# Compression's steps moved up in the last mixer of a two-block network on one core

## The chip, the cores and the metric

One core of one Trainium2 chip. The metric is the time of one execution on the device, in microseconds.

## What is computed

Two blocks run one after the other on a sequence of 256 tokens of width 1024, in float32. The first has two layers (feed-forward, hybrid mixer, feed-forward). The second has two layers of a mixer and a feed-forward; its second mixer, which the change touches, is sparse attention beside a conformer branch. Cut to what matters here:

```python
def compress_blocks(tok, pos_emb, w1, w2):
    n_cmp = (t - CMP_BLOCK) // CMP_STRIDE + 1      # blocks of 32 tokens, stride 16: 15 of them
    blocks = tok[:, :, idx] + pos_emb
    return jax.nn.gelu(blocks.reshape(...) @ w1) @ w2

def sparse_attn_conformer_mixer(h, w_in, ...):
    u = h @ w_in
    q, kc, vc, ks, vs, kw, vw, gt, cf = jnp.split(u, offs, axis=-1)
    # native_sparse_attention:
    q  = apply_rope(rms_norm(q, q_norm), cos, sin)
    ks = apply_rope(rms_norm(k_slc, k_norm[0]), cos, sin)
    kw = apply_rope(rms_norm(k_win, k_norm[1]), cos, sin)
    kc_tok = apply_rope(k_cmp, cos, sin)
    kc = rms_norm(compress_blocks(kc_tok, cmp_pos[0], cmp_w1[0], cmp_w2[0]), k_norm[2])
    vc = compress_blocks(v_cmp, cmp_pos[1], cmp_w1[1], cmp_w2[1])
    # scores of q against kc, ks, kw; softmax of each; three outputs, gated and added
    a, b = jnp.split(cf, 2, axis=-1)
    z = causal_dwconv(a * jax.nn.sigmoid(b), conf_dw) + conf_dw_b
    z = jax.nn.silu(layer_norm_2(z, conf_ln_g, conf_ln_b))
    return jnp.concatenate([o_nsa, z], axis=-1) @ w_out
```

## The kernel before

**One program, five engines.** The class Walk goes through the network once for each engine and calls the same steps in the same order; each engine's program (TensorProgram on TensorE or PE, ScalarProgram on ScalarE or ACT, VectorProgram on VectorE or DVE, GpsimdProgram on GpSimd or POOL, SyncProgram for the weight loads) issues its own part of a step, or nothing. So the place of a call in Walk is the order on every engine at once. Each engine works strictly in that order; semaphores hold a step until what it needs is there.

**Matrix products.** A float32 weight is loaded in units of 2 x 128 rows (RW, 512 KB at most), split by ACT into a high part WH (line 922) and by DVE into the rest WL (line 1266); the input has both parts too (XT), and each product is three matmuls (lines 446 to 451). These splits are called cuts. Units are loaded four ahead and cut up to five ahead (LEAD is 4); there are six places for cut units. `rows` yields after each of 8 pieces of 6 matmuls of 512 columns, `cols` with steps=2 after each of 8 pieces of 12 matmuls of 256 columns. The loop around it calls one entry of the list `beside` at each yield. So these lists set what stands between the pieces.

**The last mixer, mixer_odd.** It projects the compressed branch's keys and values, rotates the keys (`rotate("c", ...)`) and stores them to device memory (`keys_out`). `windows` (POOL, line 2095) waits for those stores, reads them back as pairs of neighbouring tokens into PRS with four loads (line 2101), and clears FB (line 2105). `paired` turns the pairs on PE (line 779) and adds the position table on DVE into FB (line 1821). `hidden` is compression's first layer: 64 matmuls on PE (line 791), Gelu on ACT (line 1179). `hidden_turn` is lines 800 and 1185, `compressed_rows` its second layer (line 825), with the norm of the compressed keys on ACT and DVE (lines 1201 to 1208, 1829 to 1838, result KCN), `compressed_keys` turns these (PE line 834, ACT line 1213, result KCT).

`rotate(kind, t, ...)` for the keys k and the queries q is a norm and a rotation: square on ACT (line 1151), sum on DVE (1781), square root on ACT (1154), six steps on DVE (1783 to 1804), two products on POOL (2072, 2074) that DVE needs at lines 1800 and 1804. `odd_q` copies q to SBUF (ACT, line 1173). `keys_double` copies the rotated keys twice into KD on POOL (line 2111); `clear_vcb` clears a table there (2116) once line 791 is done. `features` turns KD and the rotated q on PE (line 813) and copies them out on ACT (line 1192). `odd_gate` is the sigmoid of the conformer's gates, SGc (line 1160). After that a loop of ticks runs the attention items: `cmp_scores` (PE 844, DVE 1845 to 1851, exponentials on ACT, line 1221), PE 866, ACT 978, DVE 1902, PE 875, and `upper`, the conformer's upper half, whose gated result ZC (DVE, line 1811) is stored and read back shifted (POOL 2122, 2131) for the convolution (PE, line 768).

**Order around the change.** In the loop over q's eight pieces come the two rotations of k, then `windows`, then `paired(0)` and `paired(1)` at the end. In the loop over the gates' eight pieces come q's first rotation, `hidden`, `keys_double` and q's second rotation, `hidden_turn`, `features` of k, `compressed_rows`, nothing, `features("q", 0)`. `compressed_keys` is called in the second tick.

Of the kernel before, what the change touches and what calls it, by code (L numbers as in the profile page):

```python
# [2221 lines left out]
class Walk:  # L2222
# [681 lines left out]
    def mixer_odd(self):  # L2904
        k, e = self.k, self.e
# [24 lines left out]
        def rotate(kind, t, h0, h1, normed):  # L2930
            e.rotate(kind, t, h0, h1, normed, [("odd_v", ("ro", kind, 0))] if t else [])
# [7 lines left out]
        for t in range(2):  # L2939
            e.odd_win(t, bks[t])  # L2940
            self.drop(bks[t], ("odd_a", ("win", t)))

        def paired(n):
            b = self.bank()
            e.paired(n, b)
            self.drop(b, ("odd_v", ("fb", n)))

        def features(kind, t):
            b = self.bank()
            e.features(kind, t, b)  # L2950
            self.drop(b, ("odd_a", ("qkt", kind, t)))
# [17 lines left out]
        def compressed_keys():  # L2969
            b = self.bank()  # L2970
            e.cmp_keys(b)
            self.drop(b, ("odd_a", "kct"))
# [1 line left out]


        bks = [self.bank(), self.bank()]
        beside = [lambda: rotate("k", 0, 8, 12, 12), e.nothing, lambda: rotate("k", 1, 8, 12, 12), e.windows, e.nothing,
                  e.nothing, lambda: paired(0), lambda: paired(1)]
        for _ in self.rows(w, 8, 0, [(0, 512, bks)], self.x):
            beside.pop(0)()  # L2980
        for t in range(2):
# [3 lines left out]


        bks = [self.bank() for _ in range(4)]
        beside = [lambda: rotate("q", 0, 0, 8, 8), hidden, lambda: (e.keys_double(), e.clear_vcb(), rotate("q", 1, 0, 8, 8)),
                  hidden_turn, lambda: (features("k", 0), features("k", 1)), compressed_rows, e.nothing,
                  lambda: features("q", 0)]  # L2990
        for _ in self.cols(w, 1816, 4, bks, self.x, steps=2):
            beside.pop(0)()
        for j in range(4):
# [70 lines left out]
        def convolve():  # L3064
            for j in range(4):
                if j % 2 == 0:
                    b = self.bank()
                for p in range(8):
                    e.conv_taps4(j, p, b)
                    if p % 4 == 3 and 2 * j + p // 4 + 2 < 8:  # L3070
                        e.conv_weights(2 * j + p // 4 + 2)
                    if p == 7 and j % 2:
                        e.conv_sum(j - 1, b)
                        self.drop(b, ("odd_a", ("za", j)))
                    yield

        def conformer(t):
            b = self.bank()
            e.conf_turn(t, b)
            e.conf_norm(t)  # L3080
            self.drop(b, ("odd_v", ("zn", t)))
            yield
            yield
            b = self.bank()
            e.conf_back(t, b)
            self.drop(b, ("odd_a", ("zs", t)))
            yield

        def upper():

            for half in range(2):
                bks = [self.bank(), self.bank()]
                yield from self.cols(w, 1304 + 256 * half, 2, bks, self.x)
                for j in range(2):
                    e.odd_up(2 * half + j, bks[j])
                    self.drop(bks[j], ("odd_v", ("zc", 2 * half + j)))
                e.conv_out(half)
                e.conv_shift(half)
# [7 lines left out]
        up, conv, live, tick, ticks = upper(), convolve(), [], 0, 0  # L3106
        outs = 0
        while gens or live or conv:
            while gens and tick >= gens[0][0]:
                tick = 0 if gens[0][0] else tick  # L3110
                live.append(gens.pop(0)[1])
            tick += 1
            ticks += 1
            if ticks == 2:
                compressed_keys()
            if ticks == 4:
                features("q", 1)
                later["q1"] = True
            live = [g for g in live if next(g, self) is not self]
            if up:  # L3120
                if next(up, self) is self:
                    up = None
            elif conv:
                for _ in range(2):
                    if conv and next(conv, self) is self:
                        conv = None
                        live += [conformer(0), conformer(1)]
            elif outs < 4 and len(done[0]) == 4 or outs < 8 and len(done[1]) == 4:
                outs += 1
                next(y)  # L3130
# [147 lines left out]
```

## Time and profile before

| | |
|---|---|
| median of 3 runs | 2339.42 us (2338.87 to 2340.22) |
| span of the profiled execution | 2339.1 us |
| PE busy | 2277.7 us, 97% of the span |
| DVE, ACT, POOL busy | 1485.2, 1164.7, 128.7 us |
| chain that ended last, by engine | PE 86%, DVE 8%, ACT 4%, DMA 1% |

Only the span is given for the profiled execution, no time of its own; the median of the runs stands 0.3 us above that span. An engine's busy time says little by itself here. To read it: see where PE stood idle, who released it, and what that engine was doing before.

### The profile page before, as it was taken

What the parts mean: (1) busy time and instruction counts of PE and PEld (TensorE: products, weight loads), DVE (VectorE), ACT (ScalarE), POOL (GpSimd) and SP (SyncE); (2) the same over time, 40 slices, a digit from 0 to 9 for tenths busy, and PEclk for the clock granted to TensorE, in tenths of its full rate; (3) what the DMA queues carried; (4) which work ended last, traced back from release to release, by engine and by line L of the source; (5) the groups of instructions that cost most, each with busy time, mean ns of one, the idle gap of its engine ahead of it and who ended that gap; (6) DMA issues with size and microseconds to landing.
All of it is one profiled execution on the core that took longest, in us unless ns stands there. A gap on an engine that the chain in (4) does not pass through costs nothing.

```text
span 2339.1 us, 33502 instructions
## 1 busy us (share of the span) xinstructions
PE 2277.7 (97%) x13839; PEld 1929.1 (82%) x13839; DVE 1485.2 (63%) x2139; ACT 1164.7 (50%) x1799; POOL 128.7 (6%) x197
## 2 busy tenths in 40 slices
PE   8999999999999999999999999999989999788999
PEld 7888798887888878888898877888878887666887
DVE  5665567857666556664668667666467664565663
ACT  5554346534555436553356344555344553545652
POOL 2100010120000000000000110000000001320000
PEclk9999999999999999999999999999999999889999
DMA  6756473445565556566544446566535665442663
GB/s 220 228 187 214 146 226 113 133 127 188 180 191 187 190 187 199 185 203 201 175 153 132 136 145 206 180 192 209 193 122 189 182 211 175 131 129 84 205 192 132
DMA packets 283560, 408.09 MB, mean 174 GB/s; under 512 B 13700, under 2 KB 170688, under 8 KB 283152
## 3 DMA queue, kind: packets, MB, share of 16 engines
q1 hardware_dynamic: 275600, 380.91, 51.1%
q0 software_dynamic: 7808, 25.04, 3.6%
q8 instruction: 109, 1.79, 0.3%
q14 instruction: 43, 0.35, 0.0%
HBM read 403.98 MB, written 1.91 MB: 174 GB/s over the span
## 4 chain that ended last, share of the span: by engine, by line
PE 86%; DVE 8%; ACT 4%; DMA 1%; issue 1%; POOL 0%; SPq 0%; DVEq 0%; ACTq 0%; POOLq 0%
PE PS L517 23%; PE PS L449 13%; PE PS L451 12%; PE PS L450 12%; PE PS L516 10%; PE PS L446 2%; DVE WL L1266 2%; PE PS L448 2%; PE PS L447 2%; PE PS L519 1%; PE PS L466 1%; ACT WH L922 1%; DVE QX L1513 1%; DMA RW<-in_w_in_odd 1%; PE PS L661 0%
## 5 line engine op out<-in xcount | busy, mean ns | idle before, releaser
L1266 DVE TENSOR_TENSOR WL<-RW,WH 128x1024 fp32r<-128x1024 f32 (+2 forms) x732 | 870.8, 1220 | 314.9 <-ACT WH L922 312.4
L922 ACT ACTIVATE WH<-RW 128x1024 fp32r<-128x1024 f32 (+2 forms) x732 | 740.6, 1044 | 389.0 <-PE PS L451 223.2
L517 PE MATMUL PS<-XT,WH 128*128 128x512 f32 x2368 | 808.4, 394 | 0.0
L516 PE MATMUL PS<-XT,WL 128*128 128x256 f32 x2072 | 580.5, 280 | 0.0
L517 PEld LDWEIGHTS PS<-XT,WH 128*128 128x128 f32 x2368 | 425.1, 188 | 76.7
L516 PEld LDWEIGHTS PS<-XT,WL 128*128 128x128 f32 x2072 | 390.0, 188 | 13.3
L449 PE MATMUL PS<-WH,HTH 128*128 128x512 f32 x688 | 271.4, 394 | 0.0
L451 PE MATMUL PS<-WH,HTL 128*128 128x512 f32 x688 | 270.8, 394 | 0.0
L450 PE MATMUL PS<-WL,HTH 128*128 128x512 f32 x688 | 269.7, 392 | 0.0
L449 PE MATMUL PS<-WH,XT 128*128 128x512 f32 (+4 forms) x640 | 252.4, 394 | 8.5 <-DVE SX L1420 3.3
L451 PE MATMUL PS<-WH,XT 128*128 128x512 f32 (+4 forms) x640 | 243.2, 380 | 0.0
L450 PE MATMUL PS<-WL,XT 128*128 128x512 f32 (+4 forms) x640 | 242.4, 379 | 0.0
L446 PE MATMUL PS<-XT,WH 128*128 128x256 f32 x560 | 164.4, 294 | 2.5 <-DVE Z L1400 1.3
L449 PEld LDWEIGHTS PS<-WH,XT 128*128 128x128 f32 x640 | 123.3, 193 | 43.4 <-issue 10.7
L447 PE MATMUL PS<-XT,WL 128*128 128x256 f32 x560 | 158.4, 283 | 0.0
L448 PE MATMUL PS<-XT,WH 128*128 128x256 f32 x560 | 158.3, 283 | 0.0
L451 PEld LDWEIGHTS PS<-WH,HTL 128*128 128x128 f32 x688 | 129.1, 188 | 30.7
L450 PEld LDWEIGHTS PS<-WL,HTH 128*128 128x128 f32 x688 | 129.1, 188 | 30.2
L1336 DVE TENSOR_TENSOR HM<-PS,HM 128x256 f32<-128x256 f32 x148 | 62.3, 421 | 144.2 <-ACT HM L952 144.2
L449 PEld LDWEIGHTS PS<-WH,HTH 128*128 128x128 f32 x688 | 129.2, 188 | 28.9
L952 ACT ACTIVATE HM<-PS 128x256 f32<-128x256 f32 x148 | 56.8, 384 | 178.4 <-PE PS L517 174.1
L952 ACT ACTIVATE SG<-PS 128x256 f32<-128x256 f32 x148 | 56.9, 385 | 175.5 <-PE PS L517 174.7
(438 smaller groups left out, 2556.1 us busy)
## 6 DMA issues: line engine op xcount, KB each, us to landing
RW<-in_w_ff_in SPq DMA_DIRECT2D x256, 512.0 KB, 4.4
RW<-in_w_ff_out SPq DMA_DIRECT2D x128, 512.0 KB, 4.5
RW<-in_w_in SPq DMA_DIRECT2D x56, 512.0 KB, 4.5
RW<-in_w_gate SPq DMA_DIRECT2D x48, 512.0 KB, 4.2
RW<-in_ffn_gate SPq DMA_DIRECT2D x44, 512.0 KB, 4.3
RW<-in_ffn_up SPq DMA_DIRECT2D x44, 512.0 KB, 4.5
RW<-in_ffn_down SPq DMA_DIRECT2D x44, 512.0 KB, 4.6
RW<-in_w_out SPq DMA_DIRECT2D x16, 512.0 KB, 4.7
```

The lines of the kernel that those rows point to most:

```text
L446: self.e.matmul(o, wh, xh, start=start, stop=False)
L447: self.e.matmul(o, wl, xh, start=False, stop=False)
L448: return self.e.matmul(o, wh, xl, start=False, stop=stop)
L449: self.e.matmul(o, xh, wh, start=start, stop=False)
L450: self.e.matmul(o, xh, wl, start=False, stop=False)
L451: return self.e.matmul(o, xl, wh, start=False, stop=stop)
L516: self.e.matmul(k.PS[:, b.n, 0:T], wl, k.XTH[:, kt, :], start=False, stop=False)
L517: ins = self.e.matmul(k.PS[:, b.n, :], wh, k.XT[:, kt, :], start=kt == 0, stop=kt == 7)
L922: self.e.activation(u.hi_out, raw, ACT.Copy).then_inc(*self.s["hi"].up(u.n))
L952: self.e.activation(f[2 + part][:, n, j * T:j * T + T], self.k.PS[:, b.n, 0:T], ACT.Copy).then_inc(*self.s["ffn_a"].up((seq, sl, n, part, j)))
L1266: self.e.tensor_tensor(u.lo_out, raw, u.hi_out.bitcast(F), ALU.subtract).then_inc(*self.s["lo"].up(u.n))
L1336: self.e.tensor_tensor(v, self.k.PS[:, b.n, T:2 * T], v, ALU.add).then_inc(*self.s["ffn_v"].up((seq, sl, n, part, j)))
```

## The change

Five calls move; nothing is added to or taken from the work.

- `windows` is called right after the window branch's values are copied (`odd_win`), ahead of both rotations of k, where it was behind them.
- `paired(0)` and `paired(1)` come one piece earlier each, and `hidden` is called after the last piece of q, ahead of `odd_q` and of all the gates' pieces.
- `hidden_turn`, `features` of k and `compressed_rows` come one or two pieces earlier in the loop over the gates.
- `compressed_keys` is called at the end of that loop, ahead of `odd_gate`, where it was in the second tick behind it.

```diff
@@ -2939,6 +2939,7 @@
         for t in range(2):
             e.odd_win(t, bks[t])
             self.drop(bks[t], ("odd_a", ("win", t)))
+        e.windows()
 
@@ -2974,8 +2975,8 @@
         bks = [self.bank(), self.bank()]
-        beside = [lambda: rotate("k", 0, 8, 12, 12), e.nothing, lambda: rotate("k", 1, 8, 12, 12), e.windows, e.nothing,
-                  e.nothing, lambda: paired(0), lambda: paired(1)]
+        beside = [lambda: rotate("k", 0, 8, 12, 12), e.nothing, lambda: rotate("k", 1, 8, 12, 12), e.nothing, e.nothing,
+                  lambda: paired(0), lambda: paired(1), hidden]
         for _ in self.rows(w, 8, 0, [(0, 512, bks)], self.x):
             beside.pop(0)()
@@ -2985,9 +2986,9 @@
         bks = [self.bank() for _ in range(4)]
-        beside = [lambda: rotate("q", 0, 0, 8, 8), hidden, lambda: (e.keys_double(), e.clear_vcb(), rotate("q", 1, 0, 8, 8)),
-                  hidden_turn, lambda: (features("k", 0), features("k", 1)), compressed_rows, e.nothing,
-                  lambda: features("q", 0)]
+        beside = [lambda: rotate("q", 0, 0, 8, 8), hidden_turn, lambda: (e.keys_double(), e.clear_vcb(), rotate("q", 1, 0, 8, 8)),
+                  lambda: (features("k", 0), features("k", 1)), compressed_rows, e.nothing, e.nothing,
+                  lambda: (features("q", 0), compressed_keys())]
         for _ in self.cols(w, 1816, 4, bks, self.x, steps=2):
             beside.pop(0)()
@@ -3111,8 +3112,6 @@
             tick += 1
             ticks += 1
-            if ticks == 2:
-                compressed_keys()
             if ticks == 4:
```

DVE's order is the same before and after. On POOL, in the projection of q (TM are the products of k's rotation, PRS the pairs, W_150 compression's second weights):

```order
 L2083 DMA W_150<-in_cmp_w_2 128x4x64
+L2101 DMA PRS<-scratch 128x2x64 x4
+L2105 MEMSET FB_133 128x1024
+L2105 MEMSET FB_134 128x1024
 L2072 TENSOR_TENSOR TM_137<-RT_131,CO 128x128
 L2074 TENSOR_TENSOR TM_138<-RT_131,CO 128x128
 L2072 TENSOR_TENSOR TM_137<-RT_132,CO 128x128
 L2074 TENSOR_TENSOR TM_138<-RT_132,CO 128x128
-L2101 DMA PRS<-scratch 128x2x64 x4
-L2105 MEMSET FB_133 128x1024
-L2105 MEMSET FB_134 128x1024
```

The four loads and two clears pass four products.

On ACT, between q's projection and the gates' (G_140 is Gelu's output, RT the copies of q, RO their squares, SX at line 1154 the square root):

```order
 L922 ACTIVATE WH<-RW 128x2x512 x2
+L1179 ACT_TABLE_LOAD
+L1179 ACTIVATE G_140<-PS 128x256
 L1173 ACTIVATE RT_131<-PS 128x512
 L1173 ACTIVATE RT_132<-PS 128x512
 L922 ACTIVATE WH<-RW 128x2x256
 L1151 ACTIVATE RO_135<-RT_131 128x512
-L1154 ACTIVATE SX<-SX,ST 128x8
-L1179 ACT_TABLE_LOAD
-L1179 ACTIVATE G_140<-PS 128x256
```

Gelu and its table load pass both copies of q, a cut, a square and a root.

On ACT, at the end of the gates' projection (QTT is q's copy, KCT the compressed keys', SGc the gates, the table load of line 1221 is the exponentials'):

```order
 L1192 ACTIVATE QTT<-PS 128x4x128
+L1213 ACTIVATE KCT<-PS 128x64
 L1160 ACT_TABLE_LOAD
 L1160 ACTIVATE SGc<-PS 128x256 x4
 L922 ACTIVATE WH<-RW 128x2x256
-L1213 ACTIVATE KCT<-PS 128x64
 L1221 ACT_TABLE_LOAD
```

The keys' copy passes the gates and a cut.

## Rows read from the trace of the kernel before

**Rows 1.** The page's head and its busy times
```profile
span 2339.1 us, 33502 instructions
...
PE 2277.7 (97%) x13839; PEld 1929.1 (82%) x13839; DVE 1485.2 (63%) x2139; ACT 1164.7 (50%) x1799; POOL 128.7 (6%) x197
```
**Rows 2.** Timeline of PE: start, us, instruction; in brackets the idle time before it
```profile
2014.55 0.66 PE L779 MATMUL PS<-CO,PRS 128*128 128x128 f32 x2 [12.25 <-DMA PRS<-scratch]
...
2021.77 7.13 PE L791 MATMUL PS<-W,FB 128*64 128x256 f32 x64
...
2073.49 1.94 PE L768 MATMUL PS<-Z,DG 128*32 128x256 f32 x16 [4.24 <-issue]
```
**Rows 3.** Timeline of POOL
```profile
1992.59 0.75 POOL L2083 DMA_DIRECT2D W<-in_cmp_w  x1
...
2011.43 2.89 POOL L2101 DMA_DIRECT2D PRS<-scratch  x4
...
2022.35 0.96 POOL L2072 TENSOR_TENSOR TM<-RT,CO 128x256 f32<-128x256 f32 x1 [6.18 <-DVE RT L1788]
...
2023.94 1.56 POOL L2111 COPY KD<-RO 128x512 f32<-128x512 f32 x2
```
**Rows 4.** DMA issues: KB, us to landing (1989.2:1990.1, 1992.3:1993.5, 2011:2015)
```profile
scratch<-VV POOLq DMA_DIRECT2D x1, 64.0 KB, 3.9
...
W<-in_cmp_w POOLq DMA_DIRECT2D x1, 128.0 KB, 10.4
...
PRS<-scratch POOLq DMA_DIRECT2D x4, 64.0 KB, 2.5
```
**Rows 5.** Timeline of DVE
```profile
2012.08 2.35 DVE L1266 TENSOR_TENSOR WL<-RW,WH 128x1024 fp32r<-128x1024 f32 x2
2015.39 0.66 DVE L1821 TENSOR_TENSOR FB<-PS,VEC 128x480 f32<-128x480 f32 x1 [0.95 <-POOL FB L2105]
...
2025.06 0.72 DVE L1804 TENSOR_TENSOR RO<-RO,TM 128x256 f32<-128x256 f32 x1
...
2036.27 0.51 DVE L1804 TENSOR_TENSOR RO<-RO,TM 128x256 f32<-128x256 f32 x1
...
2039.11 0.29 DVE L1829 TENSOR_REDUCE SX<-KCN 128x2 f32<-128x128 f32 x1 [1.52 <-ACT KCN L1205]
...
2040.61 0.23 DVE L1838 COPY KCN<-KCN 128x128 f32<-128x128 f32 x1
```
**Rows 6.** Timeline of ACT
```profile
2020.28 0.30 ACT L1154 ACTIVATE SX<-SX,ST 128x8 f32<-128x8 f32 x1 [0.84 <-DVE SX L1781]
...
2028.95 0.38 ACT L1179 ACTIVATE G<-PS 128x256 f32<-128x256 f32 x1 [7.07 <-PE PS L791]
...
2031.68 0.30 ACT L1154 ACTIVATE SX<-SX,ST 128x8 f32<-128x8 f32 x1
...
2041.54 1.28 ACT L1160 ACT_TABLE_LOAD   x1
2042.83 1.21 ACT L1160 ACTIVATE SGc<-PS 128x256 f32<-128x256 f32 x4
...
2046.75 0.96 ACT L1221 ACTIVATE PCM<-PCM,SX 128x32 f32<-128x32 f32 x4 [0.78 <-DVE SX L1851]
...
2054.58 0.60 ACT L1192 ACTIVATE QTT<-PS 128x512 f32<-128x512 f32 x1 [0.39 <-PE PS L813]
```
**Rows 7.** Stretches: us, busy of PE, PEld, DVE, ACT, POOL, granted PE clock, DMA
```profile
2014.50:2019.90 5.40, 5.35 (x19) 4.69 (x20) 2.26 (x4) 1.63 (x3) 1.67 (x2) 0.50 0.43 123
...
2028.90:2040.90 12.00, 12.00 (x105) 12.00 (x105) 7.35 (x16) 7.86 (x17) 6.06 (x11) 1.00 0.18 45
...
2042.50:2044.80 2.30, 0.03 (x1) 0.02 (x1) 0.21 (x1) 2.27 (x8) 0.00 (x0) 1.00 0.44 112
...
2047.30:2054.10 6.80, 6.80 (x32) 6.51 (x32) 4.11 (x13) 2.32 (x8) 0.00 (x0) 0.51 0.34 126
```
**Rows 8.** The chain that ended last: start, us, what
```profile
2032.13 0.12 PE PS L446
```

## Prediction

> **What bounds the kernel now.** I read the page's busy table first, then TensorE's timeline through the last mixer, then the timelines of the three engines that it waits for, then the clock. The profiled execution spans 2339.1 us with TensorE busy 97% of it [rows 1], so only places where TensorE stands still, or runs at its lower clock, can give or take time. The last mixer has four such places [rows 2, 7]. PE waits 12.25 us before the transposes of the token pairs (line 779). It waits 2.3 us for the compressed keys before line 844. It waits 4.24 us before the conformer's convolution (line 768). And after the first two of these it works for 5.4 and 6.8 us at half the clock (granted 0.50 and 0.51, the 1.2 GHz level).
>
> The 12.25 us are a queue, not a transfer. The four loads of PRS are issued on POOL at 2011.43, because the products of the keys' rotation stand ahead of them there [rows 3]; the four landed 2.5 us after their issue at the median [rows 4]. So the change aims at a real wait. The question is what stands behind it.
>
> **The change, step by step.** No instruction is added or removed; all is order.
>
> 1. *Pairs earlier.* The loads now follow W2's load, issued at 1992.59 [rows 3]. They wait for the keys' own stores, of which the last was issued by 1990.1 and took 3.9 us [rows 4], so they begin at 1994.0. Four issues of 0.72 us, 2.89 us in all [rows 3], end at 1997.0. When they land the trace doesn't show. The nearest rows bound it: 2.5 us after issue as in a quiet time, 1999.5, and 10.4 us as W2's load took just ahead of them in the same queue, 2007.4 [rows 4]. I take 2005.5, behind W2's landing at 2003.0, since these loads stand in that queue. PE then does the two pairs' transposes and the last 12 matmuls of 512 columns in what was idle time. In turn they may delay the weight loads beside them: by nothing, or by as much as the 2.5 us that they took themselves [rows 4]. I take nothing, because they stand behind W2's load, and the weights of this stretch were asked for earlier.
>
> 2. *The hidden layer's start.* Its 64 matmuls (line 791) now follow at once, ahead of the 24 matmuls that used to stand between. But they need FB, and FB is written on DVE, whose order did not change: rotation of the keys, two cuts of weights (2012.08 and 2.35 long), then two additions of 0.66 us [rows 5]. So they start at 2014.4 + 2 x 0.66 = **2015.8**, not when the pairs land: 6.0 us sooner than 2021.77 [rows 2], not 12. PE has then waited some 6 us more and starts at the lower clock. At full clock the 64 took 7.13 us [rows 2]; as in [rows 7] I take 5.4 us at half clock, which loses 2.7. They end at 2015.8 + 7.1 + 2.7 = **2025.6**, 3.3 us sooner than 2028.9. Bounds: no loss, 2022.9, and a 6.8 us stretch, 2026.3.
>
> 3. *What the early wait on ACT costs.* Gelu (line 1179) used to stand behind the copies of q (line 1173) and the start of q's first rotation. It now stands ahead of them. ACT is in order, so it waits for line 791 before the copies, and both rotations of q, of which the first used to run beside line 791 (root at 2020.28, last DVE step ended 2025.78 [rows 5, 6]), begin after it. From Gelu to the root of a rotation took 2031.68 - 2028.95 = 2.73 us [rows 6]; two copies of q come in between, 0.6 each less an overlap of 0.1 (the copy of this size in [rows 6]), 3.73. So the root of q's first half is at 2029.4, its rotation ends 5.5 us later (as before) at 2034.9. Two DVE passes of 0.6 each (a cut and the next sum, each of about FB's size, 0.66, less their overlap) put the second root at 2036.1; that half took 2036.78 - 2031.68 = 5.1 us [rows 5, 6] and ends at 2041.2. One more cut, 0.6, and the norm of the compressed keys, 2039.11 to 2040.84, 1.73 us [rows 5]: the keys are ready at **2043.5**. Before it was 2040.84. Here the gain of step 2 is already gone.
>
> 4. *PE in that stretch.* After line 791 it has 12.0 us of work as in [rows 7] plus the 24 matmuls that moved behind it, 24 x 0.12 = 2.9 [rows 8]. In it the keys' features (line 813) are now asked for after four pieces of 12 matmuls and two transposes, 50 x 0.12 = 6.0 us, at 2031.6. They need KD from POOL, whose two copies follow q's products in order. Products 2.07 us after the root (2020.28 to 2022.35), copies 1.59 us later, 0.8 each [rows 3, 6]: first copy done at 2033.9, second at 2034.7. So PE **waits 2.3 us, then 0.4 us more**, where it waited for nothing before. Its work ends at 2025.6 + 14.9 + 2.7 = 2043.2, just ahead of the keys. But a wait of this very length, 2.30 us, was followed by a half-clock stretch that lost 3.4 us (6.8 at 0.51), and the first wait by one that lost 2.7 [rows 7]. Bounds: 0 and 3.4. I take 2.7, nearest to both: the compressed keys are turned at **2045.9**.
>
> 5. *Keys ahead of gates.* Before, ACT ran gates' table load, gates, a cut and then the keys' copy; the exponentials started at 2046.75, held by DVE and not by ACT. Now the gates stand between keys' copy and exponentials: q's copy 0.5, keys' copy 0.15 (an eighth of its size, mostly fixed cost), table load 1.28, gates 1.22, a cut of the copy's size 0.5, table load 1.28 [rows 6], 5.0 us after the turn: **2050.9**, 4.1 us later. The scores' own steps on PE and DVE fit into these 5 us and are no longer what is waited for. On from there ACT and DVE are a chain: the cut, the sums, the second exponentials, q's second copy, which had waited 0.39 us for PE [rows 6]. That slack is used up first: 4.1 - 0.4 = 3.7. This chain ends in ZC on DVE, whose transfers hold the convolution; the 4.24 us that PE waited there [rows 2] are filled by a slower PE but not by a later ZC. The work behind goes with it.
>
> A rule on ACT is worth weighing. In [rows 6] a table load starts at 2041.54, takes 1.28 us and the gates follow at 2042.83, so a switch costs 1.28. The Trainium skill ("ScalarE: Activation LUTs", What ACT_TABLE_LOAD costs) puts a switch at about 2.66 us, a drain included. By it the two switches of step 5 would bring 2.8 us more, and the sum would be 2345.9. The trace shows no drain behind the load, so the sum goes by the row.
>
> **Sum.** +3.5 us, rounded down from 3.7 for overlaps. The span of 2339.1 becomes 2342.6; the median of the runs stands 0.3 above the span, so the forecast is **2342.9 us**. A measurement of this kernel can tell about 0.2%, 4.7 us, from no change (2334.7 to 2344.1); the forecast lies inside.
>
> **Rivals.**
>
> *The clock holds* (0.20). The wait for KD is followed by no slow stretch. Then the keys, not PE, set the turn at 2043.5; exponentials at 2048.5, +1.75, less 0.4: **2340.8**. For it: the waits ahead of it are split in two. Against: the wait of the same length in [rows 7].
>
> *PE carries all* (0.12). If ACT's and DVE's order has more slack than I read, what counts is that line 791 ends 3.3 us sooner: **2336.1**; if also the slow stretch after 2047.3 goes, which lost 3.4, 2332.7. For it: PE is 97% busy. Against: q's second copy waited only 0.39 us for PE, so PE alone can't pull the rest forward.
>
> *The clock falls deep, and it is slower* (0.24). One mechanism, PE's clock after the two waits: both slow stretches last 6.8 us. Line 791 ends at 2026.3, and its followers lose 3.4 instead of 2.7: turn at 2047.3, exponentials at 2052.3, +5.5 less 0.4: **2344.5**, and to 2346.5 if the weight loads lose 2 of the 2.5 us of step 1 as well. It decides from a turn at 2046.8 on.
>
> *The pairs are late all the same* (0.04). Behind W2 and the weight loads they come after 2014.4 and the change doesn't move line 791 by all of 6.0 us; each us late is one more, say 2 us: **2344.9**. For it: DMA's share was at its full in that stretch, and W2's small load took 10.4 us. Against: the bound of 2007.4 leaves 7 us. The Trainium skill ("DMA: Bandwidth & Descriptors", Queues, rings and completion order) says each DMA engine takes turns between queues a packet at a time; by it the pairs would share with the weight loads and land sooner than I take, and this rival would be nothing. No row here shows pairs beside weight loads.
>
> **How the numbers follow.** The forecast's own case has 0.40. Faster by over 0.2% is the outer half of the second rival: 0.07. Slower by over 0.2%: all of the third, most of it beyond 2344.1, and part of the fourth: 0.25. The rest, 0.68, is within 0.2%. The range runs from 2336.5, which leaves out most of "PE carries all", to 2346.5, the third rival with its loads late.
>
> **What would show it.** Right: PRS issued near 1994 and no 12 us wait at line 779; line 791 starting within 0.5 us of 2015.8 right behind DVE's FB; Gelu followed by both copies of q at about 2025.6; a new wait of about 2.3 us of line 813 for POOL's KD; the granted clock falling after it; the exponentials (line 1221) near 2051 directly behind a table load. Wrong: line 791 starting earlier (DVE doesn't hold it), no wait at line 813, or the first exponentials at or before 2046.75. If ZC on DVE (line 1811) comes later by the amount of the total, step 5 stands; if it comes later and the total doesn't, the chain behind it had slack that I did not see.

## The result, and the profile after

The changed kernel takes **2343.09 us** (median of 12 runs, 2338.66 to 2346.19), the kernel before on the same chip 2338.85 (12 runs, 2335.46 to 2340.60). The ratio is 1.0017 with a 95% interval of 1.0010 to 1.0024: some 4 us slower, inside the 0.2% (4.7 us) that the prediction called no change, and 0.2 us from the 2342.9 predicted.

The profiled execution of the changed kernel is a short one of its 12: 2339.92 us, span 2338.1. Its last mixer also began early, for a reason ahead of the change. So places are given below from the mixer's start, the last copy of XT on ACT (line 927), to its end, the matmul on OTH (line 449) for which PE waits for DVE's last OTL (line 1451). Timelines of before and then of after, at these two places (start in us, length, engine, line, operation, tile, shape; in brackets the idle time before it and what ended it):

```profile
1982.03 0.60 ACT L927 ACTIVATE XT<-PS 128x512 fp32r<-128x512 f32 x1 [2.91 <-PE PS L466]
...
2128.49 0.51 PE L449 MATMUL PS<-WH,OTH 128*128 128x512 f32 x1 [2.60 <-DVE OTL L1451]
```

```profile
1979.45 0.60 ACT L927 ACTIVATE XT<-PS 128x512 fp32r<-128x512 f32 x1 [2.91 <-PE PS L466]
...
2127.66 0.50 PE L449 MATMUL PS<-WH,OTH 128*128 128x512 f32 x1 [2.61 <-DVE OTL L1451]
```

The stretch was 146.46 us long and is 148.21. The start moved by 2.58 us, so a time of after plus 2.58 is a time on the scale of before; such times are marked "b". First PE's timeline of after, as in [rows 2]:

```profile
2000.70 0.41 PE L779 MATMUL PS<-CO,PRS 128*128 128x128 f32 x2 [2.36 <-DMA PRS<-scratch]
...
2013.14 10.00 PE L791 MATMUL PS<-W,FB 128*64 128x256 f32 x64 [7.46 <-DVE FB L1821]
...
2031.39 1.43 PE L813 MATMUL PS<-CO,KD 128*128 128x128 f32 x8 [2.16 <-POOL KD L2111]
...
2042.04 0.38 PE L834 MATMUL PS<-CO,KCN 128*128 128x128 f32 x2
...
2059.15 0.66 PE L875 MATMUL PS<-CO,PA 128*128 128x128 f32 x4 [4.41 <-DVE PA L1902]
...
2073.12 1.51 PE L768 MATMUL PS<-Z,DG 128*32 128x256 f32 x16 [2.59 <-issue]
```

The 12.25 us wait for the pairs is 2.36 now. But PE waits 7.46 us for FB, 2.16 for KD and 4.41 for PA, where these waits were 0, 0 and 0.17 before. Line 791 starts at 2015.72b and takes 10.00 us where it took 7.13 [rows 2]. What ACT does there, as in [rows 6]:

```profile
2008.53 1.28 ACT L1179 ACT_TABLE_LOAD   x1
2023.17 0.39 ACT L1179 ACTIVATE G<-PS 128x256 f32<-128x256 f32 x1 [13.36 <-PE PS L791]
2023.45 1.08 ACT L1173 ACTIVATE RT<-PS 128x512 f32<-128x512 f32 x2
...
2026.88 0.30 ACT L1154 ACTIVATE SX<-SX,ST 128x8 f32<-128x8 f32 x1
...
2033.60 0.30 ACT L1154 ACTIVATE SX<-SX,ST 128x8 f32<-128x8 f32 x1 [4.40 <-DVE SX L1781]
...
2042.73 0.22 ACT L1213 ACTIVATE KCT<-PS 128x64 f32<-128x64 f32 x1
2042.97 1.28 ACT L1160 ACT_TABLE_LOAD   x1
2044.26 1.21 ACT L1160 ACTIVATE SGc<-PS 128x256 f32<-128x256 f32 x4
...
2047.47 0.96 ACT L1221 ACTIVATE PCM<-PCM,SX 128x32 f32<-128x32 f32 x4 [0.18 <-DVE SX L1851]
```

This is where the gain went. Gelu, at the head of ACT's queue, waits 13.36 us for line 791, and q's copies stand behind it. The root of q's first rotation is at 2029.46b; it was at 2020.28 [rows 6]. The clock, in a table of windows (length, busy time of PE, weight loads, DVE, ACT and POOL with their instructions, PE's granted clock, DMA share, GB/s):

```profile
2013.10:2018.40 5.30, 5.26 (x26) 3.34 (x28) 0.00 (x0) 0.00 (x0) 0.00 (x0) 0.50 0.20 51
...
2029.20:2031.40 2.20, 0.04 (x2) 0.01 (x1) 1.52 (x3) 0.00 (x0) 2.20 (x4) 1.00 0.00 0
2031.40:2034.50 3.10, 3.01 (x17) 2.77 (x18) 2.66 (x6) 0.90 (x3) 1.16 (x2) 0.70 0.15 19
2034.50:2037.50 3.00, 3.00 (x22) 3.00 (x21) 2.25 (x4) 0.89 (x2) 1.84 (x3) 0.74 0.22 73
...
2050.00:2054.60 4.60, 4.60 (x38) 4.25 (x36) 3.12 (x11) 1.17 (x5) 0.00 (x0) 1.00 0.38 118
2054.60:2059.10 4.50, 0.14 (x2) 0.00 (x0) 3.69 (x13) 3.80 (x13) 0.00 (x0) 1.00 0.34 117
```

Line 791 runs its first 5.3 us at 0.50, the 1.2 GHz level, behind the wait for FB. The wait for KD is followed by 6.1 us at 0.70 and 0.74. The half-clock stretch that [rows 7] show from 2047.3 on is gone; in its place stands the wait of 4.41 us.

### The profile page after: what moved, and what is told of

It reads as the page before. It is cut to its first block, busy times and chain, and to the rows that moved or that the text cites. A ratio compares the mean times of both kernels' runs of the same rounds, so it can differ in the third digit from the quotient of the medians.

```text
span 2338.1 us, 33503 instructions
## 1 busy us (share of the span) xinstructions
PE 2278.4 (97%) x13839; PEld 1930.6 (83%) x13839; DVE 1485.0 (64%) x2139; ACT 1164.3 (50%) x1799; POOL 128.8 (6%) x197
## 4 chain that ended last, share of the span: by engine, by line
PE 85%; DVE 8%; ACT 4%; DMA 1%; issue 1%; POOL 0%; SPq 0%; DVEq 0%; ACTq 0%
PE PS L517 23%; PE PS L449 13%; PE PS L451 12%; PE PS L450 12%; PE PS L516 10%; DVE WL L1266 2%; PE PS L446 2%; PE PS L447 2%; PE PS L448 2%; PE PS L519 1%; PE PS L466 1%; ACT WH L922 1%; DVE QX L1513 1%; DMA RW<-in_w_in_odd 1%; PE PS L661 0%
```

## The experiments

The theories, as the expectations name them. **A**: Gelu stands at the head of ACT's queue until line 791 ends, and q's copies and rotations behind it set the mixer's end; the early read by itself is a gain. **B**: what costs is the order of the later steps (keys' features, compressed rows and keys, gates). **C**: the early read costs, because it delays the weight loads beside it. D and E are told where they come up.

Each kernel was timed in runs that alternate with the kernel before, whose median was 2338.84, 2338.43, 2338.12 and 2338.71 in the four groups (kernels 1 to 4, 5 to 8, 9 to 11, 12). The table gives places in us after the mixer's start, read from the same rows of each profile: the last cut of the keys' weights on ACT, the start and length of line 791, the end of its wait on ACT (Gelu), the root of q's first rotation, the first ZC on DVE, the mixer's end. Last comes the median time. k0 and k1 are the keys' first and second rotation. From ZC to the end it is 68.3 to 70.7 us in all fourteen profiles, so what delays ZC delays the end. The ratios given below are those of the record. They can differ from the quotient of two medians by up to 0.05%, some 1 us; so a difference of about 1 us between two kernels says little.

| kernel | last cut | line 791 | its length | Gelu | root of q | ZC | end | median |
|---|---|---|---|---|---|---|---|---|
| before | 20.78 | 39.74 | 7.13 | 46.92 | 38.25 | 76.78 | 146.46 | 2338.85 |
| changed | 20.67 | 33.69 | 10.00 | 43.72 | 47.43 | 79.56 | 148.21 | 2343.09 |
| 1 pairs only | 20.72 | 33.83 | 9.00 | 42.86 | 34.71 | 72.79 | 143.04 | 2337.09 |
| 2 compressed keys back | 21.97 | 34.97 | 8.44 | 43.44 | 47.16 | 79.09 | 149.52 | 2343.66 |
| 3 hidden behind q's root | 22.20 | 35.22 | 9.19 | 44.45 | 36.19 | 74.62 | 142.91 | 2337.72 |
| 4 KD early | 21.65 | 35.49 | 9.61 | 45.13 | 48.84 | 79.46 | 149.22 | 2343.25 |
| 5 1 with hidden early | 21.97 | 34.98 | 10.07 | 45.09 | 48.80 | 79.75 | 149.47 | 2342.32 |
| 6 changed, k1 behind pairs | 22.03 | 31.53 | 9.45 | 41.01 | 44.72 | 76.88 | 147.46 | 2340.06 |
| 7 1, k1 behind pairs | 22.34 | 31.84 | 9.35 | 41.23 | 36.34 | 71.45 | 141.29 | 2332.85 |
| 8 changed, pairs late | 20.50 | 37.73 | 7.13 | 44.91 | 48.62 | 80.76 | 149.95 | 2342.52 |
| 9 7 with fill | 20.93 | 35.42 | 7.13 | 42.59 | 34.93 | 72.51 | 142.66 | 2337.18 |
| 10 changed with fill | 22.78 | 35.79 | 8.81 | 44.64 | 48.35 | 80.33 | 151.05 | 2342.48 |
| 11 7 with the change's rest | 21.58 | 31.07 | 8.78 | 39.88 | 35.56 | 70.07 | 139.26 | 2332.99 |
| 12 7, k0 behind pairs too | 22.18 | 28.42 | 8.81 | 38.05 | 36.44 | 68.23 | 137.34 | 2328.91 |

**1. The pairs' loads alone.** The kernel before with `e.windows()` behind odd_win:

```
+        e.windows()
-        beside = [..., lambda: rotate("k", 1, 8, 12, 12), e.windows, e.nothing,
+        beside = [..., lambda: rotate("k", 1, 8, 12, 12), e.nothing, e.nothing,
```

> Only the first part of the change: the pairs are read ahead of the keys' rotation on POOL; every other engine keeps the order of before. Theory A (the read is a real gain, and what costs is Gelu's new place on ACT ahead of q's copies): PE does 24 gate matmuls in the former wait, line 791 starts right behind DVE's FB, 6 us sooner than before, and ends 3 us sooner; q's first rotation still runs beside it. Total about -3 us against before (2336). Rival C (the early read itself costs: it delays the weight loads beside it): weight cuts on ACT come later and the total is 0 to +4 us against before.

Measured 2337.09, ratio 0.9988 (0.9980 to 0.9997). The median is 1.8 us below the kernel before; the ratio alone would say 2.8, with an interval of 0.7 to 4.7. So the early read is worth having by itself, near the 3 us of theory A, and the loss comes from the rest of the change.

**2. The compressed keys back behind the gates** (in the changed kernel):

```
-                  lambda: (features("q", 0), compressed_keys())]
+                  lambda: features("q", 0)]
...
+            if ticks == 2:
+                compressed_keys()
```

> The changed kernel with its last part undone: the compressed keys are turned in the second tick again, behind the gates' sigmoid on ACT. Theory A: with the turn as late as it is in the changed kernel, the gates fill time that ACT has anyway; the first exponentials start about 0.5 us later than in the changed kernel, total +4 to +5 us against before. Rival B (gates between keys and exponentials are the loss, as step 5 of the prediction counts them): undoing this gives back 1 us or more, total +3 us or less against before.

Measured 2343.66, ratio 1.0022 (1.0013 to 1.0031). Undoing this step gives nothing back. The first exponentials (line 1221) stand 67.54 us after the mixer's start, in the changed kernel 68.02, and the end is no sooner. PE's timeline of this kernel shows why it is even:

```profile
2046.26 1.79 PE L844 MATMUL PS<-KCT,QTT 64*128 64x32 f32 x8 [2.28 <-ACT KCT L1213]
...
2060.63 0.66 PE L875 MATMUL PS<-CO,PA 128*128 128x128 f32 x4 [0.34 <-DVE PA L1902]
```

With the keys behind the gates PE waits 2.28 us at line 844, and a window from 2046.20 to 2052.90 has a granted clock of 0.51. With the keys ahead it waits 4.41 us at line 875. The wait has only changed its place.

**3. The hidden layer behind the start of q's first rotation** (in the changed kernel):

```
-                  lambda: paired(0), lambda: paired(1), hidden]
+                  lambda: paired(0), lambda: paired(1), e.nothing]
...
-        beside = [lambda: rotate("q", 0, 0, 8, 8), hidden_turn, ...
+        beside = [lambda: (rotate("q", 0, 0, 8, 8), hidden()), hidden_turn, ...
```

> The changed kernel, but line 791 and Gelu are called behind the first piece of the gates and behind q's first rotation. Theory A: q's copies and first rotation run beside line 791 again, KD is ready early and PE doesn't wait at line 813; the compressed keys are ready 3 us sooner than in before. Total -2.5 to -3 us against before, 7 us better than the changed kernel. If the early read (C) or the gates (B) are the loss, it stays slower than before by 1 us or more.

Measured 2337.72, ratio 0.9994 (0.9985 to 1.0002): 5.4 us below the changed kernel. The root of q stands 11 us sooner after the mixer's start. The direction is as expected; the level is 1.5 us above what was expected, near that of kernel 1, and the interval includes 1.

**4. KD copied ahead of q's products on POOL** (in the changed kernel):

```
-  lambda: rotate("k", 1, 8, 12, 12), e.nothing, e.nothing,
+  lambda: rotate("k", 1, 8, 12, 12), e.keys_double, e.nothing,
...
-  lambda: (e.keys_double(), e.clear_vcb(), rotate("q", 1, 0, 8, 8)),
+  lambda: (e.clear_vcb(), rotate("q", 1, 0, 8, 8)),
```

> The changed kernel, but POOL doubles the keys into KD right behind the keys' rotation instead of behind q's products. Theory A with the clock as its second half: the 2.2 us wait of PE at line 813 goes, and with it the half-clock stretch; from then on the norm of the compressed keys on DVE sets the turn. Total 1 to 2.5 us less than the changed kernel, so +2 to +3 us against before. If the wait at line 813 is harmless: unchanged, +4 us.

Measured 2343.25, ratio 1.0018 (1.0009 to 1.0027): a miss, nothing gained. PE's timeline of this kernel:

```profile
2031.05 1.04 PE L813 MATMUL PS<-CO,KD 128*128 128x128 f32 x8
...
2042.72 0.44 PE L834 MATMUL PS<-CO,KCN 128*128 128x128 f32 x2 [2.77 <-DVE KCN L1838]
```

The wait at line 813 is gone, and no slow stretch follows it (the granted clock is 1.00 from 2031.04 to 2058.04). PE then waits 2.77 us for DVE's compressed keys instead. The turn (line 834) stands 62.68 us after the mixer's start, in the changed kernel 62.59. The weights came 1.0 us later in this profile, so at most 0.9 us can have been gained, and the times show none. In the changed kernel the keys' last step on DVE stands just ahead of the turn at 2042.04:

```profile
2041.02 0.31 DVE L1838 COPY KCN<-KCN 128x128 f32<-128x128 f32 x1
```

They were ready at 2041.33, and PE came to line 834 only 0.7 us later. So the wait for KD, with its slow clock, put the turn back by 0.7 us at most; without it DVE's keys set the turn.

**5. The hidden layer's place alone.** Kernel 1 with the hidden layer early, for which the pairs' turning also comes one piece earlier:

```
-                  e.nothing, lambda: paired(0), lambda: paired(1)]
+                  lambda: paired(0), lambda: paired(1), hidden]
...
-        beside = [lambda: rotate("q", 0, 0, 8, 8), hidden, ...
+        beside = [lambda: rotate("q", 0, 0, 8, 8), e.nothing, ...
```

> The kernel with the pairs' loads moved alone, and one more edit: the pairs one piece earlier and the hidden layer (line 791 and its Gelu) behind them, ahead of the copies of q. Keys' features, compressed rows, turn and keys stay where they were before the change. Theory A (the early Gelu on ScalarE holds back q's copies and both rotations): the root of q's first rotation stands some 12 us later after the mixer's start than with the pairs alone, and the time is 4 to 6 us above that kernel's 2337.1: 2341 to 2343.5. Theory B (what costs is the order of the keys' features, the compressed rows and the compressed keys): the time stays at 2336 to 2338.

Measured 2342.32, ratio 1.0014 (1.0005 to 1.0023): 5.2 us above kernel 1. This one step brings the loss back in full, and kernel 3, which takes it alone out of the change, removes it. The two together show that the early hidden layer is the cause. Both move line 791 on PE together with Gelu on ACT, and no run parts the two; that the loss comes by way of ACT is read from the trace, where q's copies follow Gelu's wait at once. The root of q came 14.1 us later than in kernel 1, where 12 were expected. ACT in this kernel:

```profile
2026.97 0.38 ACT L1179 ACTIVATE G<-PS 128x256 f32<-128x256 f32 x1 [13.43 <-PE PS L791]
2027.25 1.08 ACT L1173 ACTIVATE RT<-PS 128x512 f32<-128x512 f32 x2
...
2030.68 0.30 ACT L1154 ACTIVATE SX<-SX,ST 128x8 f32<-128x8 f32 x1
```

**6 and 7. FB ahead of the keys' second rotation on DVE**, in the changed kernel and in kernel 1:

```
-  lambda: rotate("k", 1, 8, 12, 12), e.nothing, ...
+  e.nothing, e.nothing, ...
-  lambda: paired(1)
+  lambda: (paired(1), rotate("k", 1, 8, 12, 12))
```

> The changed kernel with the rotation of the keys' second half asked for behind the pairs, so that VectorE adds FB (line 1821) 3.5 us sooner, ahead of that rotation. Theory A: line 791 starts 3.5 us sooner after the mixer's start (30.2 instead of 33.7), Gelu ends sooner by the same, and so both rotations of q: 3 to 4 us below the changed kernel, 2339 to 2340.5. Rival D (VectorE's own work is the bound, and what is moved ahead only delays what is behind it): within 1 us of the changed kernel's 2343.1.

> The kernel with the pairs' loads moved alone, and the rotation of the keys' second half asked for behind the pairs, so that FB comes 3.5 us sooner on VectorE. Gelu stays behind q's first rotation. Theory A: line 791 starts about 3 us sooner, Gelu too, and q's second rotation, which stands behind Gelu on ScalarE, with it: 2 to 3.5 us below the 2337.1 of the pairs alone, 2333.6 to 2335.1. Rival D (VectorE's own work is the bound): 2336.5 to 2338.

Measured 2340.06, ratio 1.0004 (0.9995 to 1.0013), and 2332.85, ratio 0.9977 (0.9967 to 0.9987): 3.0 us below the changed kernel and 4.2 below kernel 1. By the ratios the gains are 3.0 and 2.6, and the intervals of kernels 1 and 7 overlap a little. Kernel 6 is as theory A expected, kernel 7 is 0.75 us below its range. Line 791 starts 2 us sooner in each, where 3 to 3.5 were expected, though the weights came 1.4 and 1.6 us later in these profiles. In kernel 7 the root of q's first rotation is even 1.6 us later than in kernel 1. Gelu is 1.6 us sooner and the root of q's second rotation, which stands behind it, at 43.96 instead of 45.59. So it was DVE's order, not its work, that was the bound.

**8. The pairs late again** (in the changed kernel, `e.windows` back in its old slot behind the keys' second rotation):

> The changed kernel with the pairs' loads put back behind the keys' rotation on GpSimd; all else as changed. Theory A (each us by which line 791 is later holds ScalarE's queue by one more): the 12 us wait for the pairs is back, line 791 starts some 3 us later than in the changed kernel, and so does all behind Gelu: 2345.5 to 2347. Theory C (the early loads also cost, since weight loads beside them land late): the loss is smaller, 2343.5 to 2345, and the keys' rotation is 1 us sooner after the mixer's start.

Measured 2342.52, ratio 1.0016 (1.0007 to 1.0025): 0.6 us below the changed kernel, where theory A wanted some 3 more and theory C 0.4 to 1.9 more. Both ranges missed. So within the change the early read gives nothing, though it was its main step. PE's timeline and the windows of this kernel:

```profile
2011.78 0.66 PE L779 MATMUL PS<-CO,PRS 128*128 128x128 f32 x2 [13.30 <-DMA PRS<-scratch]
...
2017.32 7.13 PE L791 MATMUL PS<-W,FB 128*64 128x256 f32 x64
```

```profile
2011.78:2017.30 5.52, 5.52 (x16) 4.16 (x16) 1.32 (x2) 0.00 (x0) 1.67 (x2) 0.57 0.37 109
2017.30:2024.50 7.20, 7.20 (x66) 4.65 (x66) 0.00 (x0) 0.00 (x1) 0.00 (x0) 1.00 0.01 2
```

Line 791 starts 4.04 us later than in the changed kernel (37.73 against 33.69) but takes 7.13 us instead of 10.00. The transposes and the 12 matmuls of 512 columns now run at the low clock ahead of it. Gelu comes only 1.2 us later. And the last cut of the keys' weights, on which DVE's keys' rotation waits, is on the average of the 12 early-reading profiles at 21.75 us, in the two late-reading ones at 20.64. These 1.1 us may be the early loads' price, and 1.2 us less 1.1 would leave nothing. It is not shown: there are only two late-reading profiles, single ones of the others lie at 20.67 to 22.78, and between the two profiles compared here the cut differs by 0.2 us alone.

**9 and 10. PE's wait filled**, in kernel 7 (36 transposes) and in the changed kernel (50), ahead of line 791 (793 in these two; all lines behind it are two lower down):

```
         self.emptied(b)
+        for _ in range(36):
+            self.e.transpose(k.PS[:, b.n, tsl(0)], k.ident, k.ident)
```

> The kernel with the pairs' loads moved alone and the keys' second rotation behind the pairs, and 36 extra 128-column transposes on TensorE in its wait for FB ahead of line 791 (their result is overwritten). Theory E (that wait is paid twice, since line 791 runs at the lower clock behind it): the granted clock stays at 1.00, line 791 takes 7.1 instead of 9.35 us and Gelu comes 2 us sooner: 2330.5 to 2332. Rival (TensorE's length there is hidden by VectorE's own order): within 1 us of 2332.9.

> The changed kernel with 50 extra 128-column transposes on TensorE in its wait for FB ahead of line 791. Theory E: line 791 takes 7.1 instead of 10.0 us, Gelu, on which ScalarE's queue waits, comes 2 to 3 us sooner, and the time is 2 to 3 us below the changed kernel's 2343.1: 2340 to 2341. If the clock there costs nothing: 2342.5 to 2343.5.

Measured 2337.18, ratio 0.9990 (0.9981 to 0.9999), and 2342.48, ratio 1.0018 (1.0010 to 1.0027). Kernel 9 is slower than either of its expectations; kernel 10 misses theory E and stands at the edge of its rival. PE's timeline of kernel 9, then of kernel 10:

```profile
2011.67 5.82 PE L787 MATMUL PS<-CO 128*128 128x128 f32 x36 [3.51 <-DVE FB L1823]
2017.42 7.13 PE L793 MATMUL PS<-W,FB 128*64 128x256 f32 x64
```

```profile
2006.03 5.62 PE L787 MATMUL PS<-CO 128*128 128x128 f32 x50
...
2015.12 8.81 PE L793 MATMUL PS<-W,FB 128*64 128x256 f32 x64 [3.47 <-DVE FB L1823]
```

In kernel 9 the bank that the fill writes is freed by DVE's FB, so the fill stood behind the wait and not in it. It took over the slow clock (0.63 and 0.77 in its two halves), and line 791 behind it ran at full clock but started 3.6 us later. Gelu came 1.4 us later than in kernel 7, with the weights 1.4 us earlier: 2.8 us like for like. The medians differ by 4.3, the ratios by 3.0. In kernel 10 the fill ended 3.47 us ahead of FB, and the clock fell after all (0.57 in the 2.88 us behind that wait). Line 791 took 8.81 us; but it took 8.44 to 10.07 in the unfilled kernels with a wait of 7 us or more, so nothing is shown about what the fill gave. Whether line 791 can have its clock behind a wait filled to the end was not tried.

**11. The rest of the change on top of kernel 7** (kernel 3 with the keys' second rotation behind the pairs):

> The changed kernel with the hidden layer back behind q's first rotation and the keys' second rotation behind the pairs: so the kernel of 2332.9 with the change's other steps (pairs one piece earlier, keys' features, compressed rows and compressed keys earlier). Theory A (these steps cost and give nothing by themselves): 2332 to 2334. Theory B (they cost): 2335 or more.

Measured 2332.99, ratio 0.9981 (0.9972 to 0.9990): even with kernel 7, as theory A expected. In the profile its mixer is 2 us shorter, in the median the time is not. The earlier features, rows and keys neither cost nor bring anything that can be told.

**12. Both rotations of the keys behind the pairs** (kernel 7 with `rotate("k", 0, ...)` moved too):

```
-  beside = [lambda: rotate("k", 0, 8, 12, 12), e.nothing, ...
-            ..., lambda: (paired(1), rotate("k", 1, 8, 12, 12))]
+  beside = [e.nothing, e.nothing, ...
+            ..., lambda: (paired(1), rotate("k", 0, 8, 12, 12), rotate("k", 1, 8, 12, 12))]
```

> The kernel of 2332.9 (pairs' loads early, keys' second rotation behind the pairs) with the keys' first rotation behind the pairs as well, so that FB stands ahead of both on VectorE. Theory A: FB comes another 3.5 us sooner, TensorE has next to no wait ahead of line 791 and keeps its clock there, so line 791 takes 7.1 instead of 9.35 us; Gelu is then no longer what q's second rotation waits for: 2 to 3 us below 2332.9, 2330 to 2331. Rival D (VectorE's two rotations, which end no sooner, are the bound by now): 2332.5 to 2334.

Measured **2328.91** (5 runs, 2328.50 to 2331.61), ratio 0.9962 (0.9948 to 0.9975): 9.8 us below the kernel before (8.9 by the ratio), below every other version here, and 1.1 us below theory A's range. PE and ACT in this kernel:

```profile
2007.02 8.81 PE L791 MATMUL PS<-W,FB 128*64 128x256 f32 x64 [2.23 <-DVE FB L1821]
```

```profile
2015.04 0.30 ACT L1154 ACTIVATE SX<-SX,ST 128x8 f32<-128x8 f32 x1 [2.09 <-DVE SX L1781]
2015.36 1.28 ACT L1179 ACT_TABLE_LOAD   x1
2016.65 0.39 ACT L1179 ACTIVATE G<-PS 128x256 f32<-128x256 f32 x1
```

The table load and Gelu follow the root at once: ACT no longer waits for PE, nor PE 7 us for FB. The clock was not kept, against what was expected: behind a wait of only 2.23 us line 791 still takes 8.81. But it is off the path now.

## Why the prediction was right

Of its five steps, by the places in the profile of after:

1. *Pairs earlier.* Issued at 1994.00b, as forecast (1994.0). The issues of W2 and of the pairs on POOL, and what each took to land:

```profile
1990.04 0.75 POOL L2083 DMA_DIRECT2D W<-in_cmp_w  x1
1991.42 2.83 POOL L2101 DMA_DIRECT2D PRS<-scratch  x4 [0.63 <-DMA scratch<-VV]
...
PRS<-scratch POOLq DMA_DIRECT2D x4, 64.0 KB, 8.3
...
W<-in_cmp_w POOLq DMA_DIRECT2D x1, 128.0 KB, 9.7
```

W2 landed at 2002.3b, the first of the pairs at 2002.9b and the last at 2004.0b, where 2003.0 and 2005.5 were taken. In all twelve early-reading profiles the first pair landed 0.2 to 0.6 us behind W2 and the last 1.6 to 1.9. So the place behind W2 was right and the landing 1.5 us too late. The Trainium skill ("DMA: Bandwidth & Descriptors", Queues, rings and completion order) has each DMA engine take turns between queues a packet at a time; a landing ahead of 2005.5 agrees with it, but no run here singles that mechanism out. The price of the weight loads beside them was taken as 0, with 2.5 as the other bound. It is 0 in the profiled execution; the 1.1 us of experiment 8 are an average over twelve profiles against two, and not shown to be this price.
2. *Line 791.* Start 2015.72b against 2015.8, held by FB; end 2025.72b against 2025.6; 2.87 us lost to the clock against 2.7.
3. *ACT's queue.* Roots at 2029.46b and 2036.18b against 2029.4 and 2036.1, the second rotation's end at 2041.26b against 2041.2, the keys ready at 2043.91b against 2043.5. Kernels 3 and 5 show that the early hidden layer, whose wait on ACT this step counts, is the whole loss.
4. *KD and the clock.* The wait came, 2.16 us against 2.3. The clock behind it fell less far: 3.10 x 0.30 + 3.00 x 0.26 = 1.7 us lost against 2.7, so the turn was at 2044.62b and not at 2045.9. The step put PE 2.4 us behind the keys; it was 0.7 us behind them. Kernel 4, without this wait and its slow clock, gives nothing back that the times show. So this step was mis-sized: the keys on DVE, 0.4 us later than forecast, nearly set the turn by themselves.
5. *Gates between keys and exponentials.* From the turn to line 1221 it took 5.43 us against 5.0, so the exponentials stand at 2050.05b (2050.9). They waited the last 0.18 us for DVE, so the scores' steps did not quite fit into this time. ZC is 2.78 us late, where the sum had 3.5. Here the step's place in the sum was wrong: kernel 2 takes the gates' step back and gains nothing, since the wait then returns at line 844.

So the mechanism was right in its main part, steps 2 and 3, and that the total came within 0.2 us was in part luck. What steps 4 and 5 booked is for the most part what step 3 already cost, seen further down. And the profiled mixer is 1.75 us longer, not 3.5. The profiled execution lies 3.2 us below the median of its kernel, and what makes up these 3.2 us is not traced to a place. One sign is in the table: kernels 2, 4 and 5, which keep the early hidden layer and have nearly the same median, had their last cut 1.0 to 1.3 us later than the changed kernel's profile has it, and their mixers are 2.8 to 3.1 us longer than before.

The table load: the load of after at 2042.97 takes 1.28 us and the gates follow at 2044.26. The Trainium skill ("ScalarE: Activation LUTs", What ACT_TABLE_LOAD costs) has 2.66 us with a drain; the rows of both kernels have 1.28 with none, so the measurement decides, and the sum of 2345.9 by that rule was not reached.

Of the rivals, "the clock holds" (2340.8) was half right: the clock fell, and it cost 0.7 us at most. "PE carries all" (2336.1) falls by the result itself: line 791 ended 3.2 us sooner, and the time is 4 us longer; "deep clock" falls by the turn at 2044.62b, ahead of its 2046.8. "Pairs late" falls by the landing at 2004.0b.

## What to carry to other kernels

Before a wait is moved up in an engine's order, list what stands behind it on every in-order queue that the moved step touches. Here one Gelu put ahead of two copies and two rotations cost more than the end of a 12 us wait gave back. When a stall ends, ask who releases the next instruction: it was FB on DVE, behind two rotations that nobody was waiting for yet, and to put FB first was worth 8 us (2337.09 to 2328.91; 6 by the ratios) where the early load alone was worth 1.8 (2.8).

A profile of one execution can be 3 us off the median of its kernel. Places counted from the start of the stretch, over several kernels that share it, help to see where it differs.

## What the hardware did that was not expected

- The four loads of 64 KB landed 7.9 to 8.9 us after their issue beside the weights, where their median was 2.5 us in the kernel before. The last cut of the keys' weights stands 1.1 us later on the average of the twelve profiles with the early loads than of the two without (21.75, from 20.67 to 22.78, against 20.64); that the loads cause it is not shown.
- A short wait is enough for a slow start, and a long one need not be worse: behind 2.23 us of waiting (kernel 12; another 1.06 us ahead of line 779) line 791 took 8.81 us, behind 7.46 us 10.00, behind 10.15 us (kernel 2) 8.44, and with 5.5 us of work ahead of it 7.13. Work ahead of it takes the slow clock over; kernels 8 and 9 only moved the loss from line 791 to what stood before it.
- A slow stretch of PE beside which DVE has nearly as long a chain costs next to nothing: kernel 4 had its clock at 1.00 through that stretch, and the same time.
